# Sequence mixers of a hybrid decoder layer: a straight TensorE program and a new order of ScalarE's copies and exponentials

## The reference

```python
def mixer(h, ...):
    z = h @ w_in + b_in                        # split into q, k, v, gates of the three kinds
    hm, C1, n1, m1 = mlstm_scan(...)           # decayed scores @ v + q @ C
    hgd, Sg1 = gdn_scan(...)                   # a unit lower triangular solve per chunk and head
    hh, Sh1 = hgrn_scan(...)                   # scores with a decay of its own for each key column
    ym = head_rmsnorm(hm) * sigmoid(mo); yg = head_rmsnorm(hgd) * silu(gg); yh = head_rmsnorm(hh) * silu(hg)
    return concatenate([ym, yg, yh]) @ w_out, states

def hgrn step(S, q, k, v, lf):                 # per chunk
    G = cumsum(lf)
    attn[t, s] = sum_k q[t, k] * k[s, k] * exp(G[t, k] - G[s, k])    # s <= t
    o = (q * exp(G)) @ S + attn @ v
```

## Time and profile before

| what | us |
|---|---|
| median of 3 runs | 3810.45 |
| lowest, highest | 3802.82, 3815.51 |
| the profiled execution, its own time | 3799.49 |
| its span in the trace | 3797.7 |
| mixers of the prompt within it, from the first product of tile 0 to the end of tile 16 | about 984 to 1858 |

### The profile page before, as it was taken

The page is one execution under the profiler, slowest core; times in us unless marked ns, Lnnn a source line. Parts: engine busy times, 40 slices in busy tenths (PEclk is TensorE's granted clock), DMA queues, the critical chain, the costliest instruction groups (busy, mean ns, idle before and its releaser), DMA issues. The chain is left out here.

```text
span 3797.7 us, 52605 instructions
## 1 busy us (share of the span) xinstructions
PE 3390.8 (89%) x21605; PEld 3081.9 (81%) x21605; DVE 1817.7 (48%) x2434; ACT 1415.9 (37%) x2100; POOL 427.2 (11%) x450
## 2 busy tenths in 40 slices
PE   4899999996488888888666969999999999999998
PEld 3899999995377777777554859999999999999987
DVE  6233332121476666667445754444454454454465
ACT  6243323221344344434113533343343343343354
POOL 0000000000444444544030000000000000000000
PEclk6999999997788888888668989999999999999999
DMA  5222222325312222221205655335434335444353
GB/s 186 57 60 58 69 69 80 91 63 197 126 61 84 68 71 72 84 69 46 79 1 182 224 198 222 116 133 183 144 131 180 135 116 183 150 166 148 130 199 112
DMA packets 232380, 450.28 MB, mean 119 GB/s; under 512 B 41382, under 2 KB 115292, under 8 KB 228028
## 3 DMA queue, kind: packets, MB, share of 16 engines
q1 hardware_dynamic: 230020, 428.33, 33.9%
q10 hardware_dynamic: 2128, 18.56, 1.3%
HBM read 363.38 MB, written 83.47 MB: 118 GB/s over the span
## 5 line engine op out<-in xcount | busy, mean ns | idle before, releaser
L2757 PE MATMUL ff_p<-ff_h_hi,ff_w_hi 128*128 128x384 f32 (+1 forms) x1536 | 502.4, 327 | 24.0 <-DMA ff_h_lo<-tmp_h 24.0
L2759 PE MATMUL ff_p<-ff_h_hi,ff_w_lo 128*128 128x384 f32 (+1 forms) x1536 | 502.6, 327 | 0.0
L2758 PE MATMUL ff_p<-ff_h_lo,ff_w_hi 128*128 128x384 f32 (+1 forms) x1536 | 501.8, 327 | 0.0
L412 PE MATMUL pin_pz<-hi,pin_whi 128*128 128x424 f32 (+1 forms) x1320 | 469.2, 355 | 14.3 <-DVE pin_wlo L528 14.3
L413 PE MATMUL pin_pz<-lo,pin_whi 128*128 128x424 f32 (+1 forms) x1320 | 467.0, 354 | 0.0
L414 PE MATMUL pin_pz<-hi,pin_wlo 128*128 128x424 f32 (+1 forms) x1320 | 466.8, 354 | 0.0
L2776 PE MATMUL ff_p<-ff_w_lo,ff_f_hi 128*128 128x512 f32 (+1 forms) x1088 | 426.7, 392 | 0.0
L2777 PE MATMUL ff_p<-ff_w_hi,ff_f_lo 128*128 128x512 f32 (+1 forms) x1088 | 426.4, 392 | 0.0
L2775 PE MATMUL ff_p<-ff_w_hi,ff_f_hi 128*128 128x512 f32 (+1 forms) x1088 | 423.9, 390 | 0.0
L2860 DVE TENSOR_TENSOR ff_w_lo<-ff_w,ff_w_hi 128x1024 fp32r<-128x1024 f32 x192 | 235.2, 1225 | 344.4 <-ACT ff_w_hi L2808 344.4
L2808 ACT ACTIVATE ff_w_hi<-ff_w 128x1024 fp32r<-128x1024 f32 x192 | 203.6, 1060 | 388.1 <-PE ff_p L2777 383.8
(11 more groups left out here) (526 smaller groups left out, 5717.5 us busy)
## 6 DMA issues: line engine op xcount, KB each, us to landing
ff_w<-in_w_unit SPq DMA_DIRECT2D x192, 512.0 KB, 5.3
ff_w<-in_w_unit SPq DMA_DIRECT2D x48, 2048.0 KB, 8.0
tmp_z<-pin_z SPq DMA_DIRECT2D x32, 1024.0 KB, 5.2
mix_rb<-tmp_rows_p SPq DMA_DIRECT2D x16, 1152.0 KB, 6.7
pin_w<-in_w_in SPq DMA_DIRECT2D x33, 512.0 KB, 8.1
gat_wa<-in_w_ada ACTq DMA_DIRECT2D x8, 2048.0 KB, 29.2
mix_zb<-tmp_z SPq DMA_DIRECT2D x16, 640.0 KB, 4.4
tmp_h<-op_h_hi SPq DMA_DIRECT2D x17, 512.0 KB, 4.2
```

What stands on the lines that cost most here:

```text
L412: pe.matmul(pz[:, g, 0:n], whi[:, u, k], hi[:, k, at:at + n], start=(k == 0), stop=False)
L2757: pe.matmul(dst, w1_hi[:, u, k], hi, start=(k == 0), stop=False)
L2758: pe.matmul(dst, w1_hi[:, u, k], lo, start=False, stop=False)
L2759: mm = pe.matmul(dst, w1_lo[:, u, k], hi, start=False, stop=(k == KT - 1))
```

## The change

Four edits, all in `prompt_mixers`:

1. TensorE's bodies are written out for all 17 tiles. ScalarE, VectorE, GpSimd and SyncE keep their loops. The thresholds of TensorE's waits become constants.
2. ScalarE copies the far scores at the head of the body, before Abs and Exp of the distances, and `far_read` is raised once for each bank: the copy of `pc` waits for the first score block and its mask, the copy of `pd` for the second.
3. TensorE's `state_queries` waits for the first of the two copies, `mlstm` for the second.
4. The exponentials of the next tile: the pairs of four (heads 0-1, 2-3, 4-5) stood before `copy(3)`, `copy(4)` and `copy(5)`. Now head 0 stands before `copy(3)` and head 1 behind it, heads 2 and 3 behind `copy(4)`, head 4 before `copy(5)` and head 5 behind it.

```diff
                 def state_queries():
                     pe.wait_ge(S("gs"), b(1, 1))
-                    pe.wait_ge(S("far_read"), b(1, 1))
+                    pe.wait_ge(S("far_read"), b(2, 1))
...
                 def mlstm():
-                    pe.wait_ge(S("far_read"), b(1, 1))
+                    pe.wait_ge(S("far_read"), b(2, 2))
...
-            tiles(pe, body)
+            for t in range(TILES + 1):
+                body(t, t % 2, t // 2, first=(t == 0), last=(t >= TILES - 1), tail=(t == TILES))
...
+                if not first:
+                    for j, src in enumerate((pc, pd)):
+                        act.wait_ge(S("round"), b(2, j + 1))
+                        act.wait_ge(S("masked"), b(2, j + 1))
+                        act.activation(ps[half(0), j:HH:2, half(1)], src[half(0), :, FAR], ACT.Copy).then_inc(S("far_read"), 1)
                 if not tail:
                     hgrn_decays(t)
                 if not first:
-                    act.wait_ge(S("round"), b(2, 2))
-                    act.wait_ge(S("masked"), b(2, 2))
-                    for j, src in enumerate((pc, pd)):
-                        ins = act.activation(ps[half(0), j:HH:2, half(1)], src[half(0), :, FAR], ACT.Copy)
-                    ins.then_inc(S("far_read"), 1)
                     act.wait_ge(S("near"), b(1, 1))
...
                     if not last:
-                        decays(t + 1, 1 - u, range(0, 2))
+                        decays(t + 1, 1 - u, range(0, 1))
                     copy(3)
+                    if not last:
+                        decays(t + 1, 1 - u, range(1, 2))
                     inverse(3)
...
                 if not tail:
+                    copy(4)
                     if not last:
                         decays(t + 1, 1 - u, range(2, 4))
-                    copy(4)
                     inverse(4)
...
                     if not last:
-                        decays(t + 1, 1 - u, range(4, 6))
+                        decays(t + 1, 1 - u, range(4, 5))
                     copy(5)
+                    if not last:
+                        decays(t + 1, 1 - u, range(5, 6))
```

## The result

The changed kernel takes 3713.3 us (median of 4 runs, 3712.0 to 3714.9) against 3806.6 before (4 runs): a ratio of 0.9756, 95% interval 0.9737 to 0.9774, so 2.4% faster. The forecast was 3717, which is 93 us less than the 3810.5 of the kernel before; measured are 93.3 us less than 3806.6. The profiled execution has a span of 3710.7 us.

What follows compares the result with a forecast made beforehand. TensorE, the fullest engine, was taken to be held by waits at each tile's head and the low clock behind them. 15 x (53.7 - 47.7) = 90 us plus 3 in tile 16 gave 3810.5 - 93 = 3717, 8 in 10 from 3688 to 3760.

Steps and rivals of the forecast that it cites:

- E: Zero of a tile's times: the end of the last score product before it, 1089.19 us in tile 2's old trace.
- The idle time at the head: Head of each tile: waits for far copies and on "issue" vanish, 3.5 us per ordinary tile, 4.1 behind a jump.
- Of these 57 are idle time: Split of the 93 us saving: 57 us are TensorE's idle time, the rest mostly clock.
- The tile length of 46.9 us: A tile like tile 2 after the change: 51.45 us less 4.5, from 1089.19 to 1140.64 before.
- The new bound: `solved` (line 1868) waits 1.5 us for VectorE's line 2285 and starts at E + 7.95, against E + 12.47 before.
- a wait of over 2 us: Sign against the forecast: it is wrong if such a wait appears in every tile.
- The clock: Per tile, about 4 us at low clock around `finish` plus 2 more on average, at 0.40 us each.
- The exponentials: Around `copy(4)`: 0.6 us per tile from ending its 0.70 us wait; nothing taken at `copy(3)` and `copy(5)`.
- rival C: VectorE and GpSimd hold the tile, the scaling of `y` taking 2.91 us when it meets `bd`: 3735, chance 0.15.
- The middle of the tile: VectorE's operations on `hs` and `hq` meet GpSimd's earlier `hk`: 0.6 us lost, bounds nothing and 1.1.
- The jump: TensorE's loop jump before line 1827: 3.61 us plus 0.50 of low clock, so 4.1 us in each of five tiles.
- The sum: 15 tiles from 53.7 to 47.7 us each give 90 us, tile 16 gives 3: 93 us in all.

Runs made afterwards that it cites:

- The nine tiles in which `state_queries` starts 0.95 us later: Changed kernel with `state_queries` waiting for both far copies instead of the first: 3714.2 us, ratio 0.975 to the kernel before.
- two such edits: On the changed kernel: `rv` and its sum fused per head (3697.3 us); decays of `cm` and `gs` behind `update(1)` (3710.0 us); both together 3669.5 us, again 3665.0.

## Why the prediction was right, and where its steps were not

**The idle time at the head** went as said: both waits are gone, and `state_queries` starts at E + 0.70 (0.93 said). But "Of these 57 are idle time" was wrong: TensorE's idle time in the 15 tiles fell by 26 us. The sum had counted the waits that go and, in this sentence, not the new one of 1.5 us in each tile (22 us) that it had worked out itself; that one came out at 2.1, and a further one came for `xt`. The tile length of 46.9 us did contain the 1.5.

**The new bound** was right in place and size: `solved` at E + 7.95 as worked out, since line 2290 waits for `cl` whatever TensorE does; the wait is 2.1 us, not 1.5, because TensorE gets there at E + 5.8, not 6.4. It starts 0.2 us earlier, and lines 1847 and 1858 take 1.4 and 1.5 us, not 1.6 each; half of line 1858's 2.82 us is 1.4, so that term had been read too high. The nine tiles in which `state_queries` starts 0.95 us later and `solved` at the same E + 7.95 show the bound. The prediction named as a sign against itself "a wait of over 2 us" in every tile. This wait is one, 2.1 us in all 15, and the time came out all the same: the sign was set too sharply, for a wait of 1.5 us was expected there and TensorE's early arrival only lengthens it.

**The clock.** 6 us at low clock per tile were allowed; it is 115 / 15 = 7.7. The place was wrong. No tile has the four us around `finish` any more. Before, they followed the wait of about 1 us of line 1838 for VectorE's x, and that wait went with the new order of the exponentials. Now the stretch lies behind the wait of 2.1 us before `solved`: 8 of the first 13 tiles have 10.2 us of it, the other five 3.4 us behind the wait for `xt`. The 0.40 us per us at low clock held where it could be checked: with it the straight program alone is accounted for.

**The exponentials** were mis-sized. The step that failed is "At `copy(3)` and `copy(5)` TensorE has other work in hand while the copy is late; I take nothing". I had asked only who waits for ScalarE's copy. The pair behind `copy(5)` acts through `ex`: GpSimd's `bd` comes later and VectorE's scaling goes first. The edit is worth 20 us, not 9: with the old places line 1926 waits 9 us more for `copy(4)`, which is what I had reckoned, and line 1838 11 us more for VectorE's x, which I had not. That was rival C's own mechanism, which I had set against the forecast; with the exponentials in their old places it does happen.

**The middle of the tile.** I took 0.6 us for VectorE held up by GpSimd. It is 2.3 us in six tiles, 0.9 on average, by line 2306, an operation that I had not priced.

**The jump.** 4.1 us of idle time for each, and nothing else, was too simple. Its removal is worth 30 us by itself, of which 3 are idle time, and 15 to 23 beside the other edits, of which about 1 us for each jump is left when both kernels have the same low clock (tile 4); the rest is clock.

The sum (90 us for 15 tiles, measured 88.8) came out so close partly because these cancel: 11 us too little for the exponentials, against 5 too little for `xt` and about 10 for the clock (1.7 us more in 15 tiles at 0.40). The total of 93 came out to within a us by luck as well: the spans of the two profiled executions differ by 87.0, the medians by 93.3, with an interval of about 7 us on either side.

## What to carry to other kernels

When an engine's wait goes, work out from the next in-order engine's fixed operations when the following wait begins; that bound (here VectorE behind GpSimd) can be placed to 0.1 us from the old trace. An operation that is moved acts on everyone behind the semaphore that it raises: ask who becomes later by it too, and whom that lets pass. Shortening one of two short waits can show little, because the granted clock may still fall behind the other: here two such edits gave 0.4 and 0.15% alone and 1.1% together. Try both before judging either.

## What the runs showed of the hardware

- TensorE's clock: behind waits of 3.2 to 3.6 us at the head of a tile, low stretches of 6.8 to 23.9 us in the kernel before. Behind a wait of 2.1 us there are 10.2 us of it in nine of the changed kernel's 15 tiles and none in the other six; with VectorE's decays moved, in 14 of 15. Where the longest of these waits is 1.3 us, ten and thirteen of the 15 tiles, in two executions, have no low clock at all. TensorE is busy without a break through most of a low stretch, from 1092 to 1101 us in tile 2 of the changed kernel.
- An operation of VectorE with two SBUF operands that meets one of GpSimd is held up until that one ends: 192 columns 4.03 us instead of 0.36, 384 columns 1.74 instead of 0.55, 1024 columns 3.45 instead of 1.22. SBUF — State Buffer in the Trainium skill, section SBUF: two separate sides, states this as an exclusive lock, and the traces agree. In the kernel with both last exponentials early, GpSimd's `bd` went ahead of a scaling that the trace has as started 0.51 us before it. The same sum with one operand from PSUM was not held up: six of 64 columns took 1.23 us while `cl` ran, and line 2287 of the changed kernel, 384 columns from PSUM, 0.57.
- A taken jump of TensorE's loop: 3.2 to 3.6 us without work, each of five times, and no such wait in the straight program of 17 bodies.
